# Rounded weights at three phases of 256 bytes, and eleven gate and up slots whose weight tiles are interleaved

## The reference

```python
hn = rms_norm(h, ln_pre_ffn[layer])
gu = jnp.einsum('bld,df->blf', hn, w_gate_up[layer])
ff = jnp.einsum('blf,fd->bld', jax.nn.silu(gu[..., :D_FF]) * gu[..., D_FF:], w_down[layer])
h = h + rms_norm(ff, ln_post_ffn[layer])
```

## Time and profile before

| | us |
|---|---|
| median of 2 runs | 1710.8 |
| lowest and highest | 1710.35, 1711.25 |
| span of the profiled execution | 1708.3 |
| PE busy in it | 1687.0 |
| weight loads (PEld) busy | 1401.2 |
| VectorE busy | 1065.2 |
| ScalarE busy | 723.3 |

### The profile page before, as it was taken

The page is one execution under the profiler, slowest core; times in us unless marked ns, Lnnn a source line. Parts: engine busy times, 40 slices in busy tenths (PEclk is TensorE's granted clock), DMA queues, the critical chain, the costliest instruction groups (busy, mean ns, idle before and its releaser), DMA issues.

```text
span 1708.3 us, 21445 instructions
## 1 busy us (share of the span) xinstructions
PE 1687.0 (99%) x8588; PEld 1401.2 (82%) x8588; DVE 1065.2 (62%) x1779; ACT 723.3 (42%) x1155; POOL 154.8 (9%) x144
## 2 busy tenths in 40 slices
PE   8999999999999999999999999999999999999997
PEld 8877777888888888888888888889888888888886
DVE  7355557766665347745769665657554769667565
ACT  5436664322222237476423222535566533332533
POOL 2100000000000000111100000011211100000012
PEclk9999999999999999999999999999999999999998
DMA  4331012555554321221222222221322122222221
GB/s 178 116 112 50 26 50 87 201 196 194 197 197 160 111 99 75 99 84 65 75 99 92 97 90 94 96 99 50 124 99 75 49 99 99 97 91 90 93 99 50
DMA packets 31138, 177.49 MB, mean 104 GB/s; under 512 B 3677, under 2 KB 5869, under 8 KB 13886
## 3 DMA queue, kind: packets, MB, share of 16 engines
q1 hardware_dynamic: 22048, 144.71, 23.6%
q0 software_dynamic: 8608, 31.21, 5.3%
q10 hardware_dynamic: 382, 0.19, 0.0%
HBM read 171.28 MB, written 4.78 MB: 103 GB/s over the span
## 4 chain that ended last, share of the span: by engine, by line
PE 96%; DVE 2%; DMA 1%; ACT 1%; issue 0%; ACTq 0%; DVEq 0%
PE ps L640 29%; PE ps L642 29%; PE ps L641 28%; PE ps L1264 1%; PE ps L1252 1%; PE ps L875 1%; PE ps L905 1%; PE ps L838 1%; DVE h L1905 1%; PE ps L1099 1%; PE ps L897 1%; PE ps L678 1%; PE ps L870 0%; PE ps L836 0%; DMA w_raw<-in_w 0%; PE ps L849 0%
## 5 line engine op out<-in xcount | busy, mean ns | idle before, releaser
L640 PE MATMUL ps<-Xh,w_hi 128*128 128x512 f32 (+2 forms) x1760 | 667.0, 379 | 4.7 <-DVE y L1905 2.1
L642 PE MATMUL ps<-Xh,w_lo 128*128 128x512 f32 (+2 forms) x1760 | 655.7, 373 | 0.0
L641 PE MATMUL ps<-Xl,w_hi 128*128 128x512 f32 (+2 forms) x1760 | 655.6, 373 | 0.0
L1905 DVE TENSOR_TENSOR w_lo<-w_raw,w_hi 128x2048 fp32r<-128x2048 f32 (+1 forms) x161 | 312.2, 1940 | 252.1 <-ACT w_hi L1344 251.8
L640 PEld LDWEIGHTS ps<-Xh,w_hi 128*128 128x128 f32 x1760 | 331.8, 189 | 68.9 <-issue 10.8
L1344 ACT ACTIVATE w_hi<-w_raw 128x2048 fp32r<-128x2048 f32 (+1 forms) x158 | 260.5, 1652 | 294.1 <-DMA w_raw<-in_w 271.2
L641 PEld LDWEIGHTS ps<-Xl,w_hi 128*128 128x128 f32 x1760 | 332.0, 189 | 59.1 <-issue 2.6
L642 PEld LDWEIGHTS ps<-Xh,w_lo 128*128 128x128 f32 x1760 | 331.6, 188 | 57.9
L1912 DVE SCALAR_TENSOR_TENSOR cacc<-ain,vec,cacc 128x512 f32<-128x512 f32 x240 | 166.4, 764 | 0.0
L1344 ACT ACTIVATE gt<-ps 128x512 f32<-128x512 f32 x48 | 28.6, 596 | 200.7 <-PE ps L642 200.6
L640 PE MATMUL ps<-act_h,w_hi 128*128 128x512 f32 (+1 forms) x192 | 71.5, 373 | 1.7 <-DVE act_l L1905 1.7
(11 more groups left out here) (322 smaller groups left out, 2165.1 us busy)
## 6 DMA issues: line engine op xcount, KB each, us to landing
w_raw<-in_w SPq DMA_DIRECT2D x134, 1024.0 KB, 4.8
ada_w<-in_w_ada POOLq DMA_DIRECT2D x48, 512.0 KB, 4.7
bias_scratch<-brow POOLq DMA_DIRECT2D x2, 1312.0 KB, 6.6
h<-in_xT SPq DMA_DIRECT2D x4, 512.0 KB, 5.9
out<-h SPq DMA_DIRECT2D x8, 256.0 KB, 2.1
bias<-bias_scratch POOLq DMA_DIRECT2D x1, 1024.0 KB, 9.3
bias<-bias_scratch POOLq DMA_DIRECT2D x1, 512.0 KB, 7.4
cact<-in_c POOLq DMA_DIRECT2D x1, 512.0 KB, 6.5
```

The lines of the kernel that those rows point to most:

```text
L640: nc.tensor.matmul(o_, whi, xhi, start=start, stop=False)
L641: nc.tensor.matmul(o_, whi, xlo, start=False, stop=False)
L642: return nc.tensor.matmul(o_, wlo, xhi, start=False, stop=stop)
L1905: return nc.vector.tensor_tensor(o_, a_, b_, op)
```

## The change

The three buffers of `w_hi` are 2068 elements apart in place of 2048, so they start at 0, 80 and 160 bytes modulo 256 against `w_lo` and the moving operands; only 2048 elements of each are used. In slots 16 to 26 the tiles are interleaved in groups of f: in a group of f tiles, column c of tile i stands at c f + i. f is 2 for slots 16 and 17, 4 for 18 to 20, 8 for 21 to 23, 16 for 24 to 26. The host permutes them, and `w` gives TensorE a slice with step f, for the hi and the lo tile. `sqm` moves to the place that `cum` takes later.

```diff
+STEPS = {S_GU + 3 + i: f for i, f in enumerate((2, 2, 4, 4, 4, 8, 8, 8, 16, 16, 16))}
+ROOM = SLOT + 20
+
+
@@ -229,7 +233,7 @@
         w_raw = sb("w_raw", [P, NBUF, SLOT])
         w_lo = sb_at("w_lo", [P, NBUF, SLOT], F32R, o_wlo)
         o_whi = at[0]
-        w_hi = sb("w_hi", [P, NBUF, SLOT], F32R)
+        w_hi = sb("w_hi", [P, NBUF, ROOM], F32R)
@@ -306,7 +310,6 @@
-        sqm = sb("sqm", [P, KD, NM])
@@ -318,6 +321,7 @@
+        sqm = sb_at("sqm", [P, KD, NM], F32, o_p + 10816)
@@ -652,7 +656,13 @@
             def w(g, c0, n=P):
-                return w_hi[:, g % NBUF, c0:c0 + n], w_lo[:, g % NBUF, c0:c0 + n]
+
+                c = slice(c0, c0 + n)
+                if g in STEPS and n == P:
+                    f = STEPS[g]
+                    first = c0 // P // f * f * P + c0 // P % f
+                    c = slice(first, first + (P - 1) * f + 1, f)
+                return w_hi[:, g % NBUF, c], w_lo[:, g % NBUF, c]
@@ -2813,6 +2823,8 @@
     assert len(slots) == N_SLOTS
+    for g, f in STEPS.items():
+        slots[g] = slots[g].reshape(P, -1, f, P).swapaxes(2, 3).reshape(P, SLOT)
     return np.stack(slots)
```

## The result

The changed kernel takes 1729.86 us (median of 2 runs, 1729.47 to 1730.25) against 1710.8: slower by 1.17%, ratio 1.0117 with an interval of 1.0100 to 1.0133. Its profiled execution spans 1727.7 us, 19.4 more than before. The forecast was 1723.0 with a range of 1696 to 1744.

The account below looks back on a forecast made before the run. TensorE was taken as the bound, so only the gap between matmul starts moves time. 1708.3 + 7.0 (phases) + 5.2 (steps) = 1720.5 us of span; with 2.5 from span to median, 1723.0 us, range 1696 to 1744.

Parts of the forecast that it names:

- The floor of 215.8 ns: Gap of a 512-column float32r matmul without a stall: 512 / 2.4 + 2.5 ns, against 226.7 measured.
- Phases, +7.0: Loads of w_hi displaced by 80 or 160 bytes: 2.6 ns each on 2688 loads, +7.0 us.
- the halving of 5.1 ns to 2.6: Phases: slot 5's 5.1 ns a load halved, as every third load keeps its phase and narrow rows point the other way.
- the 2688: Count of displaced loads in the phases' term, 4/9 of all loads in the triples that count, out of 6048.
- Steps, +5.2: Interleaved slots 16 to 26: stall doubled at steps 4 to 16 (+4.7), half of that at step 2 (+0.5).
- my rival of the outlasting load: Stepped loads at three or four times their reading outlast their matmul: 1762 or 1810 us; chance 10%.
- the forecast's own case: Several ns a displaced load and a stall doubled at most: 1714 to 1733 us; chance 42%.
- Nothing moves: Rival: a load crosses the moving stream as often whatever its start and step; 1711 us, give or take 4; 18%.
- The collisions go: Rival: displaced loads need never meet the moving stream, so faster: 1695 us at half the stall, 1676 at the whole; 17%.
- Stalls by separate reads: Rival: stalls counted by memory lines, +13.7 for phases and +14.1 for steps, 1738.6 us; chance 13%.
- The cover of DVE's and ACT's work: Whole-slot operations need 1.92 and 2.29 of 10.88 us a slot, so a small change of theirs was costed at nothing.

Follow-up runs that it names:

- e11: Kernel before, with weight tiles, moving operands or both reduced to their first column repeated in slots 18 to 26: 1708.55 us beside 1708.90.
- e1: Changed kernel without interleaved slots, w_hi at 0, 80 and 160 bytes alone: 1725.56 us against 1708.61, ratio 1.0099.
- e3: Changed kernel without interleaving, w_lo and w_raw given the same 80 bytes of room a buffer as w_hi: 1729.96 us, ratio 1.0123.
- e2: Changed kernel with the three w_hi buffers in phase again, the eleven interleaved slots alone: 1715.92 us, ratio 1.0038.
- e6 to e10: Changed kernel without interleaving, w_hi's three buffers at other chosen distances modulo 256 in each run: 1731.13, 1733.11, 1732.38, 1730.86 and 1743.00 us.
- e12: Changed kernel without interleaving, all buffers in phase, whole SBUF layout 32 bytes later: 1709.82 us against 1709.86 for the kernel before, ratio 0.9998.
- e4: Kernel before, with step 4 in slot 45 alone, whose matmuls have 256 moving columns: 1718.99 us beside 1708.61.
- e5: Kernel before, with step 8 in slot 45, step 16 in slot 89, step 2 in slot 133, all 256-column matmuls: 1733.94 us beside 1709.52.

## Why the prediction was right, point by point

*What bounds.* Right. TensorE alone grew, and the time came as longer gaps between matmuls. The floor of 215.8 ns from the plain float32 rows was met exactly by e11. One thing was left out: longer gaps also shorten waits, here by 3.7 us (e1).

*Phases, +7.0.* The direction was right and so was the place, the gaps of the full-width matmuls; the size was wrong: e1 measured +17. The step that failed is the halving of 5.1 ns to 2.6. Its first reason, that every third load keeps its phase, counts the same thing twice: the 2688 are 4/9 of all loads, so the third loads had been left out of them already. The 5.1 itself was low for a displaced load: in slot 5 every fourth row stands in phase, so over the others it is an estimated 5.1 x 4/3 = 6.8. The second reason, the narrow tiles, had the right sign for them and the wrong weight: in e1 the gap of the 256-column matmuls went from 119.7 to 118.8 ns on average and that of the later full-width ones from 227.1 to 230.5, with 576 of the former and 5472 of the latter. The first block, mixed already, stayed near 232, as the step assumed. Without the halving the sum was 13.7. The measured 19.2 us on the full-width gaps are 7.9 ns for each of their 2432 displaced loads, and as e3 shows, even that is an average and not a price per load.

*Steps, +5.2.* The sum was near (3.9 beside the phases, 5.8 alone, by slots), and that is luck. I put 10.9 ns on each load of steps 4 to 16 for a doubled collision and 5 at step 2. In phase they measured 8 ns at step 4, 18 at step 8, 10 at step 16 and 6.7 at step 2: the three average 12, but by another mechanism. At steps 4 and 8 it is nearly all the load's own time, which is that of my rival of the outlasting load: twice a load's 110 ns was 220 and would have hidden under 226.7, but 233 and 240 didn't. That rival's price, a load of three or four times the length, didn't come.

*The number.* 1723.0 was forecast and 1729.86 measured, inside the range of 1714 to 1733 that I gave the forecast's own case. The two terms sum to 12.2 against 19 measured. Nearly all of the miss is the phases' term; the steps' term came near by luck.

The Trainium skill (SBUF — State Buffer, Door 1: The DMA port swizzle) has two hits on a 16-byte line as the condition for full bandwidth. The trace agrees for the load: 193 ns with two float32 on a line (step 2), 310 with one (step 4), 117 ns more. The same paragraph calls a stride of 4 float32 free, and with that the trace doesn't agree. The lines don't tell why step 8 takes another 20 or step 16 less than either, and my conversion of its lines to stalls of the moving stream, the 1738.6 us, was wrong.

*The rivals.* "Nothing moves" fell with e1. "The collisions go" fell with e2, e6 to e10: no distance and no step brought a full-width slot below the kernel before. Its condition, displaced loads under 226.7 ns, wasn't met; their slots went to 229.8 ns a matmul and more. Only the few 256-column matmuls gained, 0.8 ns each in e1. "Stalls by separate reads" had a fitting term for the phases, 13.7, and one too large for the steps. The cover of DVE's and ACT's work held: their busy times are within 0.4 us of before.

*What would have shown it.* I asked for slots at 11.5 us and displaced plain ones at 10.97; they were 11.3 to 11.8 and 11.15 on average. I also wrote that if steps differ more than phases, the stall isn't counted as I count it: steps 4, 8 and 16 span 0.47 us, the phases within each of these steps at most 0.09, so it isn't.

## What to carry to other kernels

Where a kernel is a stream of float32r matmuls of 512 columns that reload their weights, keep the weights' first column at the moving operand's address modulo 256: here that is 3 to 9 ns of 227 a matmul, and one element off already costs 4. With 256 columns the phases tried in e1 cost nothing. Keep the columns of a weight tile adjacent: under 512-column matmuls any step tried costs 7 to 18 ns, and under 256-column ones steps of 4 and more nearly double the gap, while step 2 is almost free (120 to 124 ns). When a trace has a row for a price, such as rows 6, ask first whether the count that it is multiplied by has left out the unaffected instructions already, and whether the price adds up.

## What the runs showed of the hardware

- Against the floor of 215.8 ns, a float32r stream of 512 columns stands at 10.9 ns more with an ordinary load in phase, 14 to 20 out of phase, 15 beside a load that reads one address, and 0.0 when the stream itself reads one address (e11).
- Of the 18 distances modulo 256 that were tried, only 0 gives 10.88 us; 4 bytes cost 0.21 us a slot. An odd multiple of 256 is as good as an even one: before, the `yc` inputs stand 256 bytes off `w_hi` modulo 512, and their matmuls start every 226.7 ns on average. Moving everything by 32 bytes costs nothing (e12). e3's slot at phase 0 took 10.93 us, not 10.88, with the same phases and `w_hi` 256 bytes further from `w_lo`; that, and the order among the other distances, stays open.
- Loads follow each other at 110 ns with adjacent columns (plain float32, rows 10), and under 256-column float32r matmuls at 233 at step 4, 240 at step 8 and 221 at step 16 (e4, e5). Why step 16 is cheaper than step 8 stays open.
